# Residual norms of a two-stack block kernel: sums, roots and reciprocals with tokens on partitions, spread by products, and the two units behind a norm interleaved tile by tile

## The reference, cut to what matters

```
def rms_norm(x, g):
    xf = x.astype(jnp.float32)
    y = xf * lax.rsqrt(jnp.mean(xf * xf, axis=-1, keepdims=True) + EPS)
    return (y * g.astype(jnp.float32)).astype(x.dtype)
...
    hx = rms_norm(x, g_pre) * (1.0 + scale_x) + shift_x      # first block, ahead of in_proj(hx, w_in)
...
    x = x + gate_x * rms_norm(out_x, g_post)                 # first block, behind the output product
...
        h = rms_norm_2(x, norm_g[l, 0]) * (1.0 + sc1) + sh1  # second block, ahead of h @ w_in[l]
...
        h = rms_norm_2(x, norm_g[l, 1]) * (1.0 + sc2) + sh2  # second block, ahead of h @ w_up
```

## Time and profile before

| | us |
|---|---|
| median of 3 runs | 3434.1 |
| the runs | 3421.64, 3434.1, 3435.97 |
| profiled execution, its own time | 3425.23 |
| its span | 3423.4 |
| PE busy | 3157.3 (92%) |
| DVE, ACT, POOL busy | 1512.1, 1169.3, 1042.4 |
| root and reciprocal of 128x512 | 0.69 and 3.35 |
| root and reciprocal of 128x768 | 0.90 and 4.95 |
| ten reciprocals of L2046 on RSTD (eight norms, two latent ones) | 39.9 |

### The profile page before, as it was taken

One profiled execution on the slowest core, in us unless ns is written; L12 is line 12 of the kernel. 1 busy time (PEld: TensorE's weight loads), 2 busy tenths in 40 slices (PEclk: granted clock), 3 DMA queues, 4 the chain that ended last, 5 costly groups with the idle time before them and its releaser, 6 DMA issues.

```text
span 3423.4 us, 44451 instructions
## 1 busy us (share of the span) xinstructions
PE 3157.3 (92%) x18095; PEld 2461.8 (72%) x18095; DVE 1512.1 (44%) x1800; ACT 1169.3 (34%) x1874; POOL 1042.4 (30%) x489
## 2 busy tenths in 40 slices
PE   5989899999999699888899889989999899989999
PEld 2767468888888477466677567767887677668887
DVE  3343335454221544334431377547663475644420
ACT  3235332112123335332223344544332344634432
POOL 0301003332333131023345332124554322135553
PEclk8999899999999799999999999999999999999999
DMA  4201003343222111025543221215665322023333
GB/s 175 56 13 40 1 13 99 105 117 93 62 62 61 32 38 39 1 73 161 160 116 91 79 62 44 58 44 172 187 179 155 90 56 82 2 68 99 99 93 93
DMA packets 440053, 279.71 MB, mean 82 GB/s; under 512 B 113466, under 2 KB 419244, under 8 KB 439468
## 3 DMA queue, kind: packets, MB, share of 16 engines
q1 hardware_dynamic: 439852, 276.87, 28.6%
HBM read 274.73 MB, written 2.10 MB: 81 GB/s over the span
## 4 chain that ended last, share of the span: by engine, by line
PE 61%; DVE 5%; ACT 3%; POOL 3%; issue 3%; DMA 1%; SPq 0%; ACTq 0%; DVEq 0%; POOLq 0%
PE ps L609 44%; PE ps L1048 3%; POOL WL L1890 3%; PE ps L1124 1%; PE ps L1146 1%; PE ps L1117 1%; ACT WH L1408 1%; PE ps L867 1%; PE ps L1183 1%; DVE GV L2062 1%; PE ps L871 1%; ACT PR L1484 1%; DVE RSTD L2046 1%; DVE HL L2055 1%; PE ps L652 1%
## 5 line engine op out<-in xcount | busy, mean ns | idle before, releaser
L1890 POOL TENSOR_TENSOR WL<-RAW,WH 128x1024 fp32r<-128x1024 f32 (+2 forms) x366 | 873.9, 2388 | 2049.8 <-ACT WH L1408 2044.9
L609 PE MATMUL ps<-HH,WH 128*128 128x512 f32 x2296 | 785.4, 379 | 93.5 <-DVE HL L2055 47.1
L609 PE MATMUL ps<-HL,WH 128*128 128x512 f32 x2296 | 771.6, 373 | 0.0
L609 PE MATMUL ps<-HH,WL 128*128 128x512 f32 x2296 | 769.8, 372 | 0.0
L609 PEld LDWEIGHTS ps<-HH,WH 128*128 128x128 f32 x2296 | 403.0, 191 | 205.3 <-POOL WL L1890 58.0
L1408 ACT ACTIVATE WH<-RAW 128x1024 fp32r<-128x1024 f32 (+2 forms) x366 | 377.3, 1031 | 464.7 <-PE ps L609 257.4
L609 PEld LDWEIGHTS ps<-HH,WL 128*128 128x128 f32 x2296 | 403.7, 192 | 77.4
L609 PEld LDWEIGHTS ps<-HL,WH 128*128 128x128 f32 x2296 | 403.4, 192 | 71.5 <-issue 0.7
L2114 DVE SCALAR_TENSOR_TENSOR MSUM<-RAW,CS,MSUM 128x1024 f32<-128x1024 f32 x91 | 157.4, 1755 | 24.8 <-DMA RAW<-in_w_ada 21.8
L609 PE MATMUL ps<-FH,WH 128*128 128x512 f32 x352 | 138.0, 392 | 2.8 <-POOL WL L1890 2.7
L609 PE MATMUL ps<-FL,WH 128*128 128x512 f32 x352 | 137.1, 389 | 0.0
(11 more groups left out here) (351 smaller groups left out, 5010.6 us busy)
## 6 DMA issues: line engine op xcount, KB each, us to landing
RAW<-in_w_in SPq DMA_DIRECT2D x122, 512.0 KB, 3.8
RAW<-in_w_ada SPq DMA_DIRECT2D x96, 512.0 KB, 4.0
RAW<-in_w_up SPq DMA_DIRECT2D x88, 512.0 KB, 4.6
RAW<-in_w_in SPq DMA_DIRECT2D x72, 256.0 KB, 3.7
RAW<-in_w_mod SPq DMA_DIRECT2D x32, 512.0 KB, 3.7
RAW<-in_w_down SPq DMA_DIRECT2D x32, 512.0 KB, 3.9
WMOD<-in_w_mod SPq DMA_DIRECT2D x4, 2048.0 KB, 19.0
RAW<-in_w_branch SPq DMA_DIRECT2D x16, 512.0 KB, 3.4
```

Source lines behind the costliest of these rows:

```text
L609: ins = nc.tensor.matmul(ps[0:width, t0:t0 + tn], a, b[:, k0 + k, t0:t0 + tn], start=first and k == 0 and i == 0, stop=last and k == kt - ...
L1890: nc.gpsimd.tensor_tensor(WL[s % NWS][:, 0:used], RAW[n % NRAW][:, 0:used], WH[s % NWS][:, 0:used].bitcast(F32), ALU.subtract).then_inc(*u ...
```

## The change

The sum of a norm is now made with tokens on partitions: the squared tile is stationary, 128 tokens at a time, and one column of ones moves, so that the result is one column for each 128 tokens (`column_sums`; 4 or 6 columns). ACT takes the root of these (RCOL, the first 8 columns of SMALL), DVE the reciprocal, and PE spreads them back over 128 partitions by a product of each column, repeated 128 times, with the identity (`spread_rows`), directly behind the sum in its program. `apply_norm` and "post" read this result in PSUM. The group is given back behind the last tile.

The two units behind a norm of the "pre" or "n" kind now run together (`two_units`): tile i of the first and tile i-3 of the second. They take both weight units first. ACT has a new `ahead` behind the root, which splits the weights of the second of the two, and the call behind the norm reaches one unit further. The tile RSTD2 is gone; the latent norms (qlb, kvlb) stay as they were.

```diff
+LAG = 3
@@ PE
+            def column_sums(ps, x, T, first, last):
+                for tb in range(T // P):
+                    ins = nc.tensor.matmul(ps[:, tb:tb + 1], x[:, tb * P:(tb + 1) * P], ones[:, 0:1],
+                                           start=first and tb == 0, stop=last and tb == T // P - 1)
+                return ins
             def sum_squares(key, n, sq, T):
                 ps = open_group(key)
                 for i in range(n):
                     pe.wait_ge(act_out, at(act_out, (key, "sq", i)))
-                    for t0, tn in segs(T):
-                        ins = nc.tensor.matmul(ps[:, t0:t0 + tn], ones, sq[i % 2][:, t0:t0 + tn],
-                                               start=i == 0, stop=i == n - 1)
-                    ins.then_inc(*up(product_ready, (key, "sq", i) if i < n - 1 else key))
+                    column_sums(ps, sq[i % 2], T, i == 0, i == n - 1).then_inc(
+                        *up(product_ready, (key, "sq", i) if i < n - 1 else key))
+                spread_rows(key, T)
...
+            def spread_rows(key, T):
+                pe.wait_ge(to_pe, at(to_pe, (key, "rows")))
+                ps = open_group((key, "rows"))
+                for tb in range(T // P):
+                    ins = nc.tensor.matmul(ps[:, tb * P:(tb + 1) * P], RCOL[:, tb:tb + 1].to_broadcast([P, P]), ident,
+                                           start=True, stop=True)
+                ins.then_inc(*up(product_ready, (key, "rows")))
+            def two_units(keys, loads, H, L, T, new):
+                pair = [take(key, load) for key, load in zip(keys, loads)]
+                groups = [open_group(key) for key in keys]
+                for i in range(KD + LAG):
+                    for n, k in ((0, i), (1, i - LAG)):
+                        if not 0 <= k < KD:
+                            continue
+                        if n == 0:
+                            pe.wait_ge(norm_low, at(norm_low, new(k)))
+                        w = [x[:, k * P:(k + 1) * P] for x in pair[n]]
+                        for t, (a, b) in enumerate(((w[0], H), (w[0], L), (w[1], H))):
+                            for t0, tn in segs(T):
+                                ins = nc.tensor.matmul(groups[n][:, t0:t0 + tn], a, b[:, k, t0:t0 + tn],
+                                                       start=k == 0 and t == 0, stop=k == KD - 1 and t == 2)
+                        if k == KD - 1:
+                            ins.then_inc(*up(product_ready, keys[n]))
+                            given_back(keys[n])
@@ ACT
+            def root_columns(key, T, n):
+                ps = ready(key)
+                A(RCOL[:, 0:T // P], ps[:, 0:T // P], ACT.Sqrt, bias=epsb[:, 0:1], scale=1.0 / n).then_inc(*freed(key))
...
-                root((l, "post"), T, DM, RSTD)
+                root_columns((l, "post"), T, DM)
+                ahead((l + 1, "qlb", 0) if l + 1 < DEPTH else ("2", 0, "bff", 0))
...
             def norm2(l, i):
-                root(("2", l, "n", i), SEQ, DM, RSTD2)
+                key = ("2", l, "n", i)
+                root_columns(key, SEQ, DM)
+                ahead(("2", l, "up", 0, 0) if i else ("2", l, "bff", 0))
@@ DVE
+            def inverse_columns(key, T):
+                own(key)
+                V.reciprocal(RCOL[:, 0:T // P], RCOL[:, 0:T // P]).then_inc(*up(to_pe, (key, "rows")))
...
-                inverse_root((l, "post"), RSTD, T)
+                inverse_columns((l, "post"), T)
+                rows = ((l, "post"), "rows")
+                rstd = ready(rows)
```

## The result

The changed kernel took 3446.28 us (median of 9 runs, 3434.72 to 3450.76) against 3424.03 us of the kernel before (9 runs, 3413.75 to 3435.97): ratio 1.0055, 95% interval 1.004 to 1.007. The ratio is an estimate from all the runs, not the quotient of the two medians, which lie 22 us apart. In a second measurement (e8) the ratio was 1.0048, interval 1.003 to 1.0065. By the two ratios the change costs 16 to 19 us; no change was forecast, +2.1 us and 3432 us. The measured time lies inside the stated range of 3406 to 3448, but only because the range had room for the spread of the runs.

What follows compares the result with a forecast made beforehand. PE's waits behind norms and weights (93.5 us idle) were taken as the bound. 12.8 - 3.1 - 2.3 + 11.8 - 6.0 - 5.5 - 5.6 = +2.1 us, added to the 3429.2 mean and rounded up: 3432 us, range 3406 to 3448.

Steps and rivals of the forecast that it cites:

- the pairs: Two units run together behind a norm: third unit starts 4.65 us behind the last HL; 19.0 us gained over five norms.
- PE has one tile left of the first unit: In a pair, behind the last HL: three products at 0.23 us (0.7 us) remain before the first unit is done.
- The low clock in the column sums: In pre 0, pre 1 and the seam, one-column products run at 1.2 GHz throughout: 20.2, 20.4 and 13.4 us of sums.
- The rival that the clock holds: Column products count as work and keep the full clock: sum -22 us, 3407 us, 0.6% faster; chance 0.16.
- Pre 0: First norm of layer 0: sums +8.2, chain +3.4, modulation's slow start +1.7, less 0.5 for the pair: +12.8 us.
- The chain of 3.5 us: In pre of layer 0, root, reciprocal and spread at the low clock now stand ahead of the modulation on PE.
- The seam: Post of layer 1 and n 0 of layer 0: late load and slow sums +16.9, chain -1.6, pair -3.5: +11.8 us.
- the third rival: At the seam the squares don't wait for the load: -4.7 instead of +11.8, 3415 us; chance 0.04.
- The chain from root to first use: Small root, reciprocal and spread ahead of the first GV: 1.85 or 2.6 us for 512 tokens; middle gain 2.0 us.
- The slow rival: The clock stays low through the pairs, all five lose 5.8 us: +29 us, 3461 us, 0.8% slower; chance 0.11.
- The operand in PSUM: DVE reading the inverse from PSUM costs nothing by the trace; by the skill's page about 5 us over some 80 operations.
- part 1: Root to first use behind each norm: the new chain gains 2.0 us (512 tokens) or 3.1 us (post 0).

Runs made afterwards that it cites:

- e8: The changed kernel once more, unedited, against the kernel before: ratio 1.0048, interval 1.003 to 1.0065.
- e5: Changed kernel plus one unused wide product per squared tile in pre 0, pre 1 and n 0 of layer 0: ratio 1.0154 to the kernel before.
- e3: Changed kernel without the early split of the seam's weights, left to the call behind n 0's root: ratio 0.9989 to the kernel before.
- e11: Changed kernel with only SP's queue reordered, the seam's weights loaded ahead of ROPE and its wait: ratio 0.9988 to the kernel before.
- e10: Kernel of e7 with the second unit of a pair five tiles behind the first instead of three: ratio 0.9952 to the kernel before.
- e13: Changed kernel with the first unit's last two tiles taken one behind the other in each pair: ratio 1.0039 to the kernel before.
- e7: Changed kernel with e3's edit and old wide sums, roots, reciprocals in pre 0, pre 1 and n 0 of layer 0: 0.9954 to the kernel before.

## Why the forecast missed

Two steps failed. In the norms it is the pairs, "PE has one tile left of the first unit", which together with a mis-sized chain make most of the 7 us that the gains fell short. And the time between the norms was put at nothing without a reason: 6.9 us were measured, all of it at the lower clock, and why the clock falls longer there stays open. One by one:

- *The low clock in the column sums* was right: 20.61, 20.61 and 13.78 us where 20.2, 20.4 and 13.4 stood. The rival that the clock holds is refuted. The Trainium skill (TensorE: Matmul & The Clock Gate, Part 1, "What's actually happening") says that activity releases the throttle; the windows of 46 to 52 us and of e5 disagree in that a PE that is busy all the time can stay throttled.
- *Pre 0*, +12.8 forecast, +10.0 measured. The chain of 3.5 us was right (45.19 to 48.71). The modulation lost 0.5 us and not 1.7. The root came 7.2 us later in the mean of three profiles, and not 8.2; in the first the sums began 1.2 us earlier than those of the earlier trace rows. And from the last HL to the reading of the third unit it is 28.5 us instead of 30.0, where 0.5 us of gain was forecast.
- *The seam*, +11.8 forecast, +12.6 measured: issue, landing, split and slow sums as forecast, and the third rival (no wait) is refuted by the row with 18.45 us; e3 and e11 show the cause twice.
- *The chain from root to first use* was mis-sized in the accumulated norms. I took the middle of 1.85 and 2.6 us on the ground that PE comes from dense products; it was 2.71 us in nearly all of n 0 and n 1, since a spread of 8 records took 2.08 us there (n 1 of layer 0), as at the low clock. The gain is 1.5 and not 2.0 us. In n 1 of layer 0 some of the column products ahead of the root were slow too in two profiles of three: last square to root 3.88 instead of 2.83 us in the first. In post 1 the chain took 1.79, 2.71 and 1.79 us, so there the middle was about right.
- *The pairs*, 19.0 us forecast behind five norms, measured 14.5 in the first profiles. The third unit was read, counted from the last HL, at 10.7 to 11.2 us instead of 13.9 to 14.7, and in n 1 of layer 0 at 13.05 instead of 15.42. The step that failed is "PE has one tile left of the first unit": it has two, with a tile of the second between them (e10, e13). The third unit starts 5.3 us behind the last HL in n 0 and n 1, 0.65 us later than forecast, and 4.9 us behind it in pre 1. The rest lies in n 1 of layer 0, where ACT's next split waits for its load ahead of reading the third unit (the row at 2344.34, 1.92 us idle for RAW); there I had counted the start of the unit and not its end.
- *The slow rival*, clock low through the pairs: it was back near 2333, 6 us behind the first HL (2326.32 + 0.75), with 4 us of tiles to come, and a lag that frees PE from the second unit brought nothing (e10).
- *The operand in PSUM* (part 1) cost nothing, as the rows had it: 1.53 us for two GV, where all in SBUF took 1.54. The Trainium skill (VectorE: DVE Perf Modes, section on the TRN2 errata) gives DVE a longer fixed term from PSUM; for these shapes the trace disagrees.
- *The sum.* The four stretches with gains came in 7 us short and the seam 1 us worse, pre 0 was 3 us better: +7.2 in place of +2.1. Another 7 us lie between the norms. Together they carry the time from no change across the bound of 0.5%. That bound was too wide as well: with the runs taken here the intervals reach 0.15 to 0.2% to either side, so a change of 0.5% can be told from none.
- *Luck.* Pre 0 came out 2.8 us better for reasons that the forecast did not have, which hid over half of what the pairs fell short of.

## What to carry to other kernels

Before a wait is put into a queue, look at the strict queue behind it: a split that depends on a load costs nothing or 16 us by the order of two loads. A sum by one-column products saves root and reciprocal but here it paid in TensorE's clock where PE summed alone, for 96 or 64 records on end (e7 against e3: 11.8 us in the norms); where DVE accumulates and few such products are left it gained some 1.5 to 3 us a norm. Cut the span at rows that both kernels have: that separated 7 us which belong to the change from as much that moves from run to run.

## What the runs showed of the hardware

- One-column products with a weight load of 128x128 kept PE busy without a gap for 20.6 us while the granted clock stayed at 0.50. So it did over the 34 us of e5's sum (25.12 to 59.39), a mix with wide products, 1.84 of each 4.27 us. With wide products alone, at the same place, the 32 records took 12.98 us, and the clock was at 1.00 from 30 us on (e7).
- Between the norms the clock fell at most of the long bursts of one-column products (those of the earlier trace rows) and at none of the short ones. In the three profiles of the kernel before, it fell in or within 1.3 us of the end of 10 of the 12 bursts of 32 records (3.6 to 4.8 us each), and neither in nor within 4 us of any of the 36 bursts of 16 records (1.84 us each). Which of the long ones it spares differs from execution to execution.
- A record of a column product took 0.215 us at the low clock, one of the spread (128 columns) 0.244 us at the low clock (2.93 / 12) and 0.145 us at the upper one (1.16 us for the 8 of post 1, at 1949.20). A 128x512 product in 32 bits took 1.84 us at the low clock (e5).
- The same stretch of an unchanged program took 62.0 or 68.6 us, by whether the clock fell in it.
